# Column-group products with a fold for the first modulation blocks and the sums of squares, in a one-step diffusion backbone

## The reference

```python
def rms_norm(x, w):
    y = xf * lax.rsqrt(jnp.mean(xf * xf, axis=-1, keepdims=True) + NORM_EPS)
    return (y * w.astype(jnp.float32)).astype(x.dtype)

def modulate(h, shift, scale):
    return h * (1.0 + scale) + shift
...
'mod_w': nrm((DEPTH, D, 6 * D), 0.5 * D ** -0.5),   # and mod_b (DEPTH, 6 * D)
```

## Time and profile before

| | us |
|---|---|
| runs of the kernel | 2290.08 median of 3 (2285.47 to 2293.35) |
| profiled execution, its time | 2292.88 |
| its span, first to last instruction | 2291.1 |
| PE busy | 2115.6 (92%) |
| PEld busy | 1828.8 (80%) |
| DVE busy | 1223.9 (53%) |
| ACT busy | 691.6 (30%) |
| POOL busy | 275.2 (12%) |
| mean granted TensorE clock | 0.962 of full speed |

### The profile page before, as it was taken

One profiled execution on the slowest core, in us unless ns is written; L12 is line 12 of the kernel. 1 busy time (PEld: TensorE's weight loads), 2 busy tenths in 40 slices (PEclk: granted clock), 3 DMA queues, 4 the chain that ended last, 5 costly groups with the idle time before them and its releaser, 6 DMA issues.

```text
span 2291.1 us, 48310 instructions
## 1 busy us (share of the span) xinstructions
PE 2115.6 (92%) x20674; PEld 1828.8 (80%) x20674; DVE 1223.9 (53%) x2483; ACT 691.6 (30%) x1187; POOL 275.2 (12%) x376
## 2 busy tenths in 40 slices
PE   6999888889899999999899978888979999999996
PEld 6666667886699999999775756887759989899995
DVE  5565764444366423323464855545166666666664
ACT  1111133431232122121211033342044454544542
POOL 0000305530000000000000213551000110101110
PEclk8999989999989999999999978999999999999998
DMA  6443301000233322210344211000145666666666
GB/s 237 153 166 110 115 1 42 6 5 1 74 111 142 116 75 74 74 65 29 117 152 137 84 68 40 7 4 3 37 163 201 217 199 217 201 216 217 205 204 197
DMA packets 190641, 256.58 MB, mean 112 GB/s; under 512 B 9152, under 2 KB 141712, under 8 KB 190256
## 3 DMA queue, kind: packets, MB, share of 16 engines
q1 hardware_dynamic: 185440, 237.32, 30.0%
q0 software_dynamic: 4992, 16.13, 2.8%
HBM read 239.26 MB, written 16.78 MB: 112 GB/s over the span
## 4 chain that ended last, share of the span: by engine, by line
PE 83%; DVE 8%; issue 3%; ACT 3%; POOL 1%; DMA 1%; SPq 0%; DVEq 0%; POOLq 0%
PE bank L942 43%; PE bank L933 11%; PE bank L1208 9%; PE bank L1450 6%; PE bank L1087 3%; PE bank L894 2%; PE bank L915 2%; PE bank L1176 1%; PE bank L1193 1%; PE bank L1164 1%; ACT arena L1620 1%; DVE arena L2320 1%; DVE rms L1926 1%; DVE arena L2224 1%; PE bank L988 1%
## 5 line engine op out<-in xcount | busy, mean ns | idle before, releaser
L942 PE MATMUL bank<-g_hi,w_hi 128*128 128x224 f32 (+1 forms) x1376 | 393.5, 286 | 10.2 <-issue 10.1
L942 PE MATMUL bank<-g_lo,w_hi 128*128 128x224 f32 (+1 forms) x1376 | 392.4, 285 | 0.0
L942 PE MATMUL bank<-g_hi,w_lo 128*128 128x224 f32 (+1 forms) x1376 | 391.2, 284 | 0.0
L2056 DVE TENSOR_TENSOR w_lo<-ring,w_hi 128x1024 fp32r<-128x1024 f32 x192 | 232.3, 1224 | 134.0 <-ACT w_hi L1857 134.0
L933 PE MATMUL bank<-arena,ring 128*128 128x320 f32 (+1 forms) x1024 | 287.4, 440 | 10.3 <-ACT arena L1620 10.0
L1208 PE MATMUL bank<-arena 64*64 64x64 f32 (+1 forms) x8640 | 261.3, 226 | 32.3 <-issue 15.8
L1208 PEld LDWEIGHTS bank<-arena 64*64 64x64 f32 x8640 | 245.3, 134 | 46.5 <-issue 22.2
L942 PEld LDWEIGHTS bank<-g_hi,w_hi 128*128 128x128 f32 x1376 | 265.1, 193 | 12.2 <-issue 11.7
L933 PEld LDWEIGHTS bank<-arena,ring 128*128 128x128 f32 (+1 forms) x1024 | 191.3, 189 | 95.0 <-issue 13.3
L942 PEld LDWEIGHTS bank<-g_lo,w_hi 128*128 128x128 f32 x1376 | 265.2, 193 | 0.2
L942 PEld LDWEIGHTS bank<-g_hi,w_lo 128*128 128x128 f32 x1376 | 265.1, 193 | 0.0
(11 more groups left out here) (284 smaller groups left out, 2869.3 us busy)
## 6 DMA issues: line engine op xcount, KB each, us to landing
ring<-in_moe_w SPq DMA_DIRECT2D x100, 1024.0 KB, 7.0
arena<-in_mod_w SPq DMA_DIRECT2D x32, 1024.0 KB, 5.3
ring<-in_ffn_w SPq DMA_DIRECT2D x30, 1024.0 KB, 7.4
ring<-in_mod_w SPq DMA_DIRECT2D x16, 1024.0 KB, 7.1
ring<-in_w_in SPq DMA_DIRECT2D x16, 1024.0 KB, 7.5
ring<-in_w_out SPq DMA_DIRECT2D x8, 1024.0 KB, 8.7
ring<-in_dft SPq DMA_DIRECT2D x4, 1024.0 KB, 7.0
ring<-in_w_in SPq DMA_DIRECT2D x4, 896.0 KB, 10.9
```

Source lines behind the costliest of these rows:

```text
L942: ins = mm(out, lhs[x], rhs[y], start=(first and i == 0), stop=(last and i == 2))
L2056: v.tensor_tensor(dst[1], src, f32(dst[0]), ALU.subtract).then_inc(s_lo2, 1)
```

## The change

* The constants are reordered so that `fold` and `eps` come with the first transfer.
* SP asks for x first, in three transfers (context, two halves of the latent tokens), then for the parameters, then for modulation blocks 0 to 3 into four buffers of their own (`mod_first`), then for the first projection weights, then for the tables. Blocks 0 to 3 no longer pass through `ring`.
* Blocks 0 to 3 of layer 0 are products in four column groups (`mod_parts`): stationary is silu(c) padded to 32 columns (`silu_pad`, cleared by GpSimd), moving are 512 weight columns. One bank holds four partial sums; ACT (blocks 0, 2) or DVE (1, 3) copies it to `mod_part`, and `mod_folds` sums the groups with four small products. TensorE makes them after the transposes of x and the first products of the squares.
* In all four norms the sums of squares are made in the same form (`square_parts`, 32 columns of ones stationary); ACT copies out the first half, DVE the second, and one product with ones for each half (`sum_squares`) gives the sums, 32 times too large, which the root's scale takes back.
* `first_tiles` runs the first four projection tiles (eight halves, eight banks) with the model block k outermost.
* VectorE sums half-blocks 8 and 9 right after the scaling of h, into two buffers; half-block 8 is multiplied out behind the first four tiles, 9 to 12 behind tiles 5 to 8, 13 to 16 behind QKV tiles 0 to 3. The wait for the tables moves from before the norm to before the QKV tiles.

```diff
-            for s in FIRST_SUBS[:4]:
-                order.add(("ms", 0, s), "V")
             for j in range(NT):
                 for q in range(2):
                     order.add(("x", j, q), "AV"[q])
-            for s in FIRST_SUBS[4:]:
-                order.add(("ms", 0, s), "V")
+        for h in range(2):
+            order.add(("sp1", l, h), "AV"[h])
+        if l == 0:
+            for i in range(MOD_FIRST):
+                order.add(("mp", i), "AV"[i % 2])
+                if i > 0:
+                    order.add(("mf", i - 1), "V")
+            order.add(("mf", MOD_FIRST - 1), "V")
         for h in range(2):
             order.add(("ss1", l, h), "A")
         for n, (name, _, _) in enumerate(RW_TILES):
             for h in range(2):
                 order.add(("in", l, name, h), "A" if name[0] in ("wa", "gd") else "AV"[h])
-            if n > 0:
...
+            sp.dma_start(x_in[:, 0, :], a["x_prompt"][0]).then_inc(s_x, 16)
+            for q in range(2):
+                sp.dma_start(x_in[:, 1 + 2 * q:3 + 2 * q, :], a["x_sample"][0].rearrange("(j p) n -> p j n", p=P)[:, 2 * q:2 * q + 2, :]).then_inc(s_x, 16)
...
                 if l == 0:
-                    load(("mod", l, 0))
-                    load(("mod", l, 1))
-                    sp.dma_start(x_in[:, 0, :], a["x_prompt"][0]).then_inc(s_x, 16)
-                    sp.dma_start(x_in[:, 1:NT, :], a["x_sample"][0].rearrange("(j p) n -> p j n", p=P)).then_inc(s_x, 16)
+                    for i in range(MOD_FIRST):
+                        src = a["mod_w"][0].rearrange("(k p) n -> p k n", p=P)[:, :, 512 * i:512 * (i + 1)]
+                        for q in range(2):
+                            sp.dma_start(mod_first[i][:, 4 * q:4 * q + 4, :], src[:, 4 * q:4 * q + 4, :]).then_inc(s_modf[i], 16)
+                    load(("win", l, 0))
                     sp.dma_start(const[:, first:NCONST], a["const"][:, first:NCONST]).then_inc(s_tables, 16)
-                    load(("mod", l, 2))
-                    load(("mod", l, 3))
                 sp.wait_ge(s_zero, l + 1)
...
-                load(("win", l, 0))
+                if l > 0:
+                    load(("win", l, 0))
...
-            def sum_squares(name, l, nth):
+            def grouped(b, stationary, moving, ready=None):
+
+                for x in range(2):
+                    for g in range(4):
+                        k = 4 * x + g
+                        if ready:
+                            ready(k)
+                        m = moving(k)
+                        ins = mm(b[32 * g:32 * g + 32, 0:m.shape[1]], stationary(k), m, start=(x == 0), stop=(x == 1),
+                                 tile_position=(0, 32 * g), skip_group_check=True)
+                return ins
+
+            def square_parts(n, l, nth):
                 for h in range(2):
-                    b = psum[order.open(pe, (name, l, h))]
-                    for k in range(KT):
-                        if h == 0:
-                            pe.wait_ge(s_sq, KT * (nth - 1) + k + 1)
-                        ins = mm(b[:, 0:HALF], ones, hT[:, k, HALF * h:HALF * (h + 1)], start=(k == 0), stop=(k == KT - 1))
-                    end(ins)
+                    b = psum[order.open(pe, (f"sp{n}", l, h))]
+                    end(grouped(b, lambda k: ones[:, 0:32], lambda k: hT[:, k, HALF * h:HALF * (h + 1)],
+                                (lambda k: pe.wait_ge(s_sq, KT * (nth - 1) + k + 1)) if h == 0 else None))
+
+            def sum_squares(n, l):
+                for h in range(2):
+                    order.wait_emptied(pe, (f"sp{n}", l, h))
+                    b = psum[order.open(pe, (f"ss{n}", l, h))]
+                    end(mm(b[:, 0:HALF], ones, rs[:, HALF * h:HALF * (h + 1)], start=True, stop=True))
+
+            def mod_parts(i):
+
+                pe.wait_ge(s_modf[i], 32)
+                b = psum[order.open(pe, ("mp", i))]
+                end(grouped(b, lambda k: silu_pad[:, k, :], lambda k: mod_first[i][:, k, :]))
+
+            def mod_folds(i):
+
+                order.wait_emptied(pe, ("mp", i))
+                b = psum[order.open(pe, ("mf", i))]
+                for t in range(4):
+                    ins = mm(b[:, 2 * t:2 * t + 2], mod_part[:, i, P * t:P * t + P], cst("fold", 2), start=True, stop=True)
+                end(ins)
...
+            def first_tiles(l):
+
+                wait_item(pe, ("win", l, 0))
+                w = view(ring, item(("win", l, 0)), KT, 512)
+                groups = [(name, col, h) for name, _, col in RW_TILES[:4] for h in range(2)]
+                banks = [psum[order.open(pe, ("in", l, name, h))] for name, _, h in groups]
+                for k in range(KT):
+                    pe.wait_ge(s_h, KT * 2 * l + k + 1)
+                    for b, (_, col, h) in zip(banks, groups):
+                        ins = mm(b[:, 0:HALF], w[:, k, col:col + P], hT[:, k, HALF * h:HALF * (h + 1)],
+                                 start=(k == 0), stop=(k == KT - 1))
+                        if k == KT - 1:
+                            end(ins)
...
-                    pe.wait_ge(s_silc, 1)
-                    for n in FIRST_SUBS[:4]:
-                        mod_sub(l, n)
-                    pe.wait_ge(s_x, 32)
+                    pe.wait_ge(s_x, 48)
                     for j in range(NT):
                         for q in range(2):
                             b = psum[order.open(pe, ("x", j, q))]
                             for k in range(4):
                                 ins = tr(b[:, P * k:P * k + P], x_in[:, j, P * (4 * q + k):P * (4 * q + k) + P], ident)
                             end(ins)
-                    for n in FIRST_SUBS[4:]:
-                        mod_sub(l, n)
+                square_parts(1, l, 2 * l + 1)
+                if l == 0:
+                    pe.wait_ge(s_silc, 1)
+                    for i in range(MOD_FIRST):
+                        mod_parts(i)
+                        if i > 0:
+                            mod_folds(i - 1)
+                    mod_folds(MOD_FIRST - 1)
+                sum_squares(1, l)
+                first_tiles(l)
+                mod_sub(l, SUB_FIRST)
+                in_tiles(l, RW_TILES[4:], SUB_FIRST + 2)
                 if l == 0:
                     pe.wait_ge(s_tables, 16)
-                sum_squares("ss1", l, 2 * l + 1)
-                in_tiles(l, RW_TILES, SUB_FIRST)
...
-                    if j in (0, 3):
-                        mod_sub(l, SUB_FIRST + (7 if j == 0 else 8))
+                    if j < 4:
+                        mod_sub(l, SUB_FIRST + 5 + j)
...
                         order.wait_emptied(act, ("out", l, k, 1))
                     ac(hT[:, k, :], xT[:, k, :], ACT.Square).then_inc(s_sq, 1)
+                b = take((f"sp{which}", l, 0))
+                end(ac(rs[:, 0:HALF], b[:, 0:HALF], ACT.Copy))
+                if l == 0 and which == 1:
+                    for i in range(0, MOD_FIRST, 2):
+                        b = take(("mp", i))
+                        end(ac(mod_part[:, i, :], b[:, :], ACT.Copy))
                 for h in range(2):
                     b = take((f"ss{which}", l, h))
-                    end(ac(rs[:, HALF * h:HALF * (h + 1)], b[:, 0:HALF], ACT.Sqrt, scale=1.0 / D, bias=cst("eps", 1)))
+                    end(ac(rs[:, HALF * h:HALF * (h + 1)], b[:, 0:HALF], ACT.Sqrt, scale=1.0 / (32 * D), bias=cst("eps", 1)))
...
+            def first_mods(l):
+
+                if l == 0:
+                    for i in range(MOD_FIRST):
+                        if i % 2 == 1:
+                            b = take(("mp", i))
+                            end(v.tensor_copy(mod_part[:, i, :], b[:, :]))
+                        if i > 0:
+                            mod_fold(i - 1)
+                    mod_fold(MOD_FIRST - 1)
+                    order.wait_emptied(ve, ("mf", MOD_FIRST - 1))
+                else:
+                    order.wait_emptied(ve, ("ms", l, SUB_FIRST - 1))
+                m = 2 * SUB_FIRST
+                chain.did(v.tensor_tensor(mod[:, 0:m, :], mod[:, 0:m, :], par[:, 0:m][:, :, None].broadcast_to([P, m, 2]),
+                                          ALU.add))
+                chain.settle()
+
+            def mod_fold(i):
+
+                b = take(("mf", i))
+                end(v.tensor_copy(mod[:, 4 * i:4 * i + 4, :], b[:, 0:8].rearrange("p (t v) -> p t v", v=2)))
...
-                    ve.wait_ge(s_silc, 1)
-                    for i in range(0, SUB_FIRST, 4):
-                        mod_sums(0, i)
-                        mod_sums(0, i + 1)
-                        for n in FIRST_SUBS[i:i + 4]:
-                            mod_take(0, n)
-                        if i == 0:
-                            for j in range(NT):
-                                b = take(("x", j, 1))
-                                end(v.tensor_copy(xT[:, 4:8, P * j:P * j + P], b[:, :].rearrange("p (k t) -> p k t", k=4)))
+                    for j in range(NT):
```

(32 more changed lines are left out.)

82 lines of the change are left out of this document (39 added, 43 removed).

## The result

| | runs | median, us | lowest to highest |
|---|---|---|---|
| before, with the changed kernel | 3 | 2290.08 | 2285.47 to 2293.35 |
| changed kernel | 3 | 2264.90 | 2255.92 to 2271.23 |

The ratio is 0.9889 with a 95% interval of 0.9853 to 0.9924: faster by 1.1%. The profiled execution is the slowest of the three, 2271.23 us (span 2269.0, mean granted clock 0.956); the other two have 0.967 and 0.958. What of the 10 us is a wrong step, and what is this one execution, is the question of the experiments.

What follows compares the result with a forecast made beforehand. TensorE was taken as the bound (83% of the span), with a serial start in which no engine is full. Gains of 28.2 + 1.0 + 0 + 6.0 = 35.2 us turn 2292.88 into 2258, 2255 as a median; range 2247 to 2270.

Steps and rivals of the forecast that it cites:

- part 2: First four projection tiles with model block outermost: 1.0 us saved over both layers, bounds -0.7 to +2.8 in each.
- part 4: The three norms after layer 0's first: 7.4 us from last square to scaled h, 6.0 us saved in sum.
- Part 1: Start of layer 0, modulation blocks 0 to 3 as column-group products: scaled h 28.2 us earlier, bounds 17 to 30.
- The relay: Start of layer 0 as a serial chain: x arrives, transposes, squares, blocks, folds, closing products, root, two reciprocals, scaled h.
- the all-fast 40.7: Time in us of layer 0's first scaled h if TensorE's start runs wholly at the upper clock level.
- the 42.5: Forecast time in us of layer 0's first scaled h, with the first block slow and the others fast.
- Rival E: Start of layer 0: transfers bound it; at 300 GB/s the last block lands at 40.5, total 2262 us; chance 0.05.
- A: Start of layer 0: TensorE stays at the lower clock until the first tiles; gain 22 us, total 2268; chance 0.17.
- B: Start and norms: column groups with full weight blocks run one behind another; gain 3.3 us, total 2287; chance 0.05.
- C: QKV stage: VectorE becomes the bound, some 0.5 us at each of six waits, 3 us; total 2258; chance 0.05.
- D: Projections: TensorE stays at the lower clock, making the kernel slower, 2325 us at 70 us of such work; chance 0.02.
- the forecast's three signs of being wrong: A block's weights landing later than 35 us, folds taking 2 us each, or first tiles running long at half clock.

Runs made afterwards that it cites:

- the repeat: The changed kernel run and profiled once more with no edit: median 2259.54 us over six runs, ratio 0.9858 to the kernel before; its profiled execution took 2259.33 us.
- the early roots: Against the changed kernel, layer 0's first norm has its closing products, roots and reciprocals issued ahead of the last modulation blocks: 2259.96 us.

## Why the prediction was nearly right

*The sum.* By rows of the repeat: scaled h 70.66 - 43.65 = 27.0 us earlier (forecast 28.2), part 2 0.4 (1.0), part 4 5.9 (6.0); 33.3 us against a forecast of 35.2. The two profiled executions differ by 2292.88 - 2259.33 = 33.6. That this agrees with the sum is partly luck: in the repeat's profile the attention stretches of the two layers are 2.0 and 1.8 us longer than before and the experts 1.1, and other stretches without an edit are shorter by about as much. The medians moved less, by 25.2 us in the first series and 29.4 in the repeat's. The median of the repeat's series, 2259.54, is 4.5 above the forecast, that of the first series 10.

*Part 1.* The relay was right, its beginning was not. In the repeat the parameters landed at 11.9 us instead of 10.5, the transposes of x took 7.01 us instead of 5.8, and the last square ended at 25.4 instead of 22.5: 2.9 us late. Of that, 1.4 us are the arrival, which had left out that the 13 small transfers are issued one by one behind x until 6.9 us, and 1.2 are the pace of the transposes: 26 of the 40 began 0.21 us apart and the others, from 17.7 us on, 0.11, where in the 5.78 us of the earlier trace rows only 13 were slow. The windows view of TensorE's transposes (busy PE and PEld, clock, DMA) on either side of 17.7 us in the repeat:

```profile
12.50:17.50 5.00, 5.00 (x25) 5.00 (x24) 1.00 1.04 390
17.80:19.00 1.20, 1.20 (x13) 1.20 (x12) 1.00 1.04 386
```

The clock column reads 1.00 for both, but the trace's records of the clock begin only at 17.7 us, with the upper level; that the slow ones ran at the lower one is an inference from the factor of two. From the last square on the estimate is good to a few tenths: 1.85 us a block (1.8), 0.94 to 0.98 a fold (0.9), 4.18 for two reciprocals (4.32). The 1.8 us that I had added to the all-fast 40.7 for a slow first block was not needed in that execution, where the clock reads 1.00 from 20 to 40 us. So the mis-sized terms are the arrival and the transposes on one side, and the clock of the first block on the other; that h came within 1.2 us of the 42.5 is partly their offset.

*The weights.* 390 GB/s flowed from 15 to 35 us, not 409, which costs 1.3 us by the time block 3 is in. It was in time in the repeat; in the first profile it landed at 34.61 and TensorE waited 1.10. By the estimate from the 358 GB/s of the Trainium skill, DMA: Bandwidth & Descriptors, Specifications, it would have landed at 34.6. The landing agrees in that one execution, the flow does not in either. Rival E (transfers bound the start) was thus true for 1.1 us of one execution, and the early roots show how little hangs on it: 4.45 us came out of the line behind the blocks.

*The other rivals.* A, the lower clock throughout the start: no, but its last third in the first profile, for 3.15 us together with block 3. B, column groups one behind another: no, 1.85 us for 16 records. C, VectorE in QKV: no waits. D, a low clock through the projections: tiles of 8.72 us as before. None of the forecast's three signs of being wrong came, though two were near in the first profile: the last block landed at 34.6 us (35), and a fold took 1.75 (2).

*Part 2.* A gain of 0.4 us over the old tiles where 2.8 a layer were possible at most: in the repeat 64 products take 37.6 us where 34.9 would be full speed. As weighed, the slow first microseconds now stand in the open: the clock reads 0.50 from the first of them, at 45.9, to 50 us.

*What no term had.* The time behind the edits was taken as fixed. It is not: the same instructions of layer 0's attention took 57.4 us at a clock of 0.74 in one execution and 66.1 at 0.63 in another, and the kernel's nine runs lie between 2246.86 and 2271.23. And an edit that changes the number of TensorE's instructions can cost 15 us in the experts, 1,600 us later. By luck the change left that alone (549.5 and 550.0 us); with 124 instructions more, the measured gain would have been nil (2284.94 to 2286.34), though 11 of those 25 us are the added instructions themselves.

## What to carry to other kernels

A serial start can be read off a profile to a microsecond or two when each step's size stands in another row, but time the first transfers with everything that is queued in front of them. Compare stages, not totals, when single parts of a change are undone: the total here moved by 7 to 16 us in stages whose code was the same. Where a long loop stands behind the edited code, look at TensorE's waits for nothing that the profile shows at the turns, before and after the edit, set them beside the times of the instruction transfers, and try moving the code by a part of 256 instructions.

## What the runs showed of the hardware

- At each turn of the experts' loop TensorE stood 1.8 to 2.3 us, until 2.8 to 2.9 us after a transfer of 16 KB of instructions had begun. Where the pass ran out of the transferred instructions after 5 or 6 products, it stood another 1.4 to 2.5 us for the next transfer.
- Where the code of this loop lies in TensorE's stream was worth 15 to 17 us in 550: a rest of 19 to 57 or of 134 (of 256) was good, 163 cost 6 us and 181 or 182 about 16, about half of it by the lower clock behind the pauses.
- An instruction that only waits for a signal long given takes TensorE 0.1 us.
- Sixteen column-group records of 512 columns take 1.85 us, in four groups, at the upper clock level; 2.56 us in a stretch where the level fell.
- Products that nobody uses, put into waits, raised the granted clock of layer 0's attention stretch from 0.74 to 0.86 and shortened it by less than 1 us; in layer 1 they raised it from 0.67 to 0.79 and 0.84, and the stretch took 59.7 and 56.0 us instead of 61.7.
